# Moving each left operand of the matmuls off the multiple of 512 bytes at which it starts

## The reference, cut to what matters

```
x = x + (u * (W_s v + b)) @ w_out        # u, v = halves of gelu(rms_norm(x) @ w_in), v layer-normed
x = x + (silu(h @ w_gate) * (h @ w_up)) @ w_down          # h = rms_norm(x), width 5632 inside
k, v = rms_norm(h @ w_k), h @ w_v                          # 16 heads of 128
x = x + softmax(q k^T) v @ w_o                             # causal, q = rms_norm(rms_norm(x) @ w_q)
x = x + (silu(h @ w_gate) * (h @ w_up)) @ w_down
```

## Time and profile before

| | |
|---|---|
| median of 3 runs | 2164.18 us (2164.0 to 2165.37) |
| profiled execution: its time | 2164.16 us |
| profiled execution: span, first to last instruction | 2162.4 us |
| busy: PE, PEld | 2140.1 us, 1777.0 us |
| busy: VectorE, ScalarE | 1117.8 us, 998.6 us |
| granted TensorE clock, mean | 0.998 of full |
| instructions | 25371 |

### The profile page before, as it was taken

One profiled execution on the slowest core, in us unless ns is written; L12 is line 12 of the kernel. 1 busy time (PEld: TensorE's weight loads), 2 busy tenths in 40 slices (PEclk: granted clock), 3 DMA queues, 4 the chain that ended last, 5 costly groups with the idle time before them and its releaser, 6 DMA issues.

```text
span 2162.4 us, 25371 instructions
## 1 busy us (share of the span) xinstructions
PE 2140.1 (99%) x9745; PEld 1777.0 (82%) x9745; DVE 1117.8 (52%) x1222; ACT 998.6 (46%) x1229; POOL 29.6 (1%) x37
## 2 busy tenths in 40 slices
PE   7999999999999999999999999999999999999999
PEld 6888888888888888888888888788888888888887
DVE  4566554455444544444556565554554445544443
ACT  5444554444444444444566565454444444443332
POOL 0000000000000000000000000000000000000000
PEclk9999999999999999999999999999999999999999
DMA  8555555555555555554654444455555555555553
GB/s 292 195 165 186 175 186 187 191 194 191 179 193 194 187 182 195 195 192 145 228 188 163 167 167 152 156 195 193 187 186 191 189 186 188 193 188 191 193 193 131
DMA packets 202057, 402.47 MB, mean 186 GB/s; under 512 B 6576, under 2 KB 6672, under 8 KB 201744
## 3 DMA queue, kind: packets, MB, share of 16 engines
q1 hardware_dynamic: 200896, 398.53, 54.4%
q10 hardware_dynamic: 1104, 3.15, 0.4%
HBM read 399.56 MB, written 2.10 MB: 186 GB/s over the span
## 4 chain that ended last, share of the span: by engine, by line
PE 98%; DMA 0%; DVE 0%; issue 0%; ACT 0%; SPq 0%; POOL 0%; ACTq 0%; DVEq 0%
PE acc L904 31%; PE acc L908 31%; PE acc L906 31%; PE tr L931 2%; DMA res<-in_x_dram 0%; PE tr L975 0%; PE tr L1049 0%; PE tr L1039 0%; PE tr L1057 0%; PE acc L931 0%; PE tr L1067 0%; PE tr L1066 0%; PE tr L1048 0%; PE tr L1065 0%; ACT w_hi L342 0%
## 5 line engine op out<-in xcount | busy, mean ns | idle before, releaser
L633 DVE TENSOR_TENSOR w_lo<-raw,w_hi 128x1024 fp32r<-128x1024 f32 x656 | 801.5, 1225 | 873.4 <-ACT w_hi L342 872.8
L342 ACT ACTIVATE w_hi<-raw 128x1024 fp32r<-128x1024 f32 x656 | 692.8, 1060 | 937.8 <-PE acc L908 937.8
L904 PE MATMUL acc<-w_hi,a_hi 128*128 128x512 f32 x2048 | 806.4, 394 | 3.5 <-DVE w_lo L633 3.5
L908 PE MATMUL acc<-w_hi,a_lo 128*128 128x512 f32 x2048 | 799.0, 390 | 0.0
L906 PE MATMUL acc<-w_lo,a_hi 128*128 128x512 f32 x2048 | 798.7, 390 | 0.0
L904 PEld LDWEIGHTS acc<-w_hi,a_hi 128*128 128x128 f32 x2048 | 385.5, 188 | 82.8 <-issue 3.8
L908 PEld LDWEIGHTS acc<-w_hi,a_lo 128*128 128x128 f32 x2048 | 385.4, 188 | 80.9
L906 PEld LDWEIGHTS acc<-w_lo,a_hi 128*128 128x128 f32 x2048 | 385.7, 188 | 78.6
L904 PE MATMUL acc<-w_hi,h_hi 128*128 128x512 f32 x704 | 274.3, 390 | 0.0
L908 PE MATMUL acc<-w_hi,h_lo 128*128 128x512 f32 x704 | 274.0, 389 | 0.0
L906 PE MATMUL acc<-w_lo,h_hi 128*128 128x512 f32 x704 | 273.9, 389 | 0.0
(11 more groups left out here) (110 smaller groups left out, 775.5 us busy)
## 6 DMA issues: line engine op xcount, KB each, us to landing
raw<-in_ffn_w_gate_dram SPq DMA_DIRECT2D x88, 1024.0 KB, 5.0
raw<-in_ffn_w_up_dram SPq DMA_DIRECT2D x88, 1024.0 KB, 5.0
raw<-in_ffn_w_down_dram SPq DMA_DIRECT2D x88, 1024.0 KB, 4.9
raw<-in_a_w_in_dram SPq DMA_DIRECT2D x32, 1024.0 KB, 5.2
raw<-in_a_w_out_dram SPq DMA_DIRECT2D x16, 1024.0 KB, 4.9
raw<-in_w_v_dram SPq DMA_DIRECT2D x16, 1024.0 KB, 4.9
raw<-in_w_k_dram SPq DMA_DIRECT2D x16, 1024.0 KB, 4.9
raw<-in_b_w_q_dram SPq DMA_DIRECT2D x16, 1024.0 KB, 4.8
```

Of the source, the lines that this page charges most:

```text
L342: nc.scalar.activation(dst, src, ACT.Copy).then_inc(hi_split, 1)
L633: nc.vector.tensor_tensor(lo, src, hi, ALU.subtract).then_inc(lo_split, 1)
L904: nc.tensor.matmul(acc[s][t][:, :], hi[:, kb, tok], w_hi[:, slot, k, :], start=kb == 0, stop=False)
L908: ins = nc.tensor.matmul(acc[s][t][:, :], lo[:, kb, tok], w_hi[:, slot, k, :], start=False, stop=kb == HG * n - 1)
```

## The change

Tiles named `pad0` to `pad7`, which nothing reads or writes, are put ahead of each left operand, and the filler `edge_high` is made 256 bytes smaller. No instruction is added, removed or moved; only start addresses change:

| left operand | start, bytes past a multiple of 512: before | after |
|---|---|---|
| a_hi, a_lo | 0, 0 | 128, 256 |
| g_hi, g_lo | 0, 0 | 32, 320 |
| h_hi, h_lo | 0, 0 | 384, 448 |
| o_hi, o_lo | 0, 0 | 96, 224 |

`raw`, `w_hi` and `w_lo` stay where they were. What is allocated behind a pad moves with it: `res`, `stage` and `ident` to 256, `v_nat`, `ln_gain`, `ln_bias`, `w_sT` and `u_nat` to 320, and `val`, `k_nat`, `q_nat`, `kT`, `qT`, `prob` and the others of the attention to 224. Each of the three parts behind `edge_high` begins at the same byte as before, since 256 bytes were added ahead and 256 taken from the filler.

```
+        pads = iter(range(16))
+
+        def pad(size, scope=ctx):
+            sb(f"pad{next(pads)}", [P, size // 4], F32, scope)
+
         sb("edge_low", [P, (-FIRST % LINE) // 4], F32)
         raw = sb("raw", [P, RAW, 2 * HG, CH], F32)
         w_hi = sb("w_hi", [P, RING, HG, CH], F32R)
         w_lo = sb("w_lo", [P, RING, HG, CH], F32R)
+        pad(128)
         a_hi = sb("a_hi", [P, KB, S], F32R)
+        pad(128)
         a_lo = sb("a_lo", [P, KB, S], F32R)
         res = sb("res", [P, TT, D], F32)
...
-        sb("edge_high", [P, (-SMALL % LINE) // 4], F32)
+        sb("edge_high", [P, (-SMALL - 256) % LINE // 4], F32)
...
+            pad(32, part)
             g_hi = sb("g_hi", [P, KB, S], F32R, part)
+            pad(288, part)
             g_lo = sb("g_lo", [P, KB, S], F32R, part)
...
+            pad(384, part)
             h_hi = sb("h_hi", [P, FB, S], F32R, part)
+            pad(64, part)
             h_lo = sb("h_lo", [P, FB, S], F32R, part)
...
+            pad(96, part)
             o_hi = sb("o_hi", [P, KB, S], F32R, part)
+            pad(128, part)
             o_lo = sb("o_lo", [P, KB, S], F32R, part)
```

## The result

| | before | changed |
|---|---|---|
| median | 2164.16 us (2164.0 to 2165.37, 4 runs) | 2218.72 us (2217.04 to 2219.24, 4 runs) |
| profiled span | 2162.4 us | 2215.3 us |
| granted TensorE clock | 0.998 | 0.999 |

What follows compares the result with a forecast made beforehand. The prediction took TensorE's 9024 large matmuls, 226.7 ns each from start to start, to bound the kernel. All terms were 0, so 2164.16 + 0 = 2164.2 us; own range 2160 to 2168, 8-in-10 range 2132 to 2206.

Steps and rivals of the forecast that it cites:

- The sum and what bounds: Whole kernel: TensorE's 9024 large matmuls at 226.7 ns decide; the change adds 0 to 2164.16 us.
- the terms for the small matmuls, ScalarE, VectorE and the DMAs: Work besides the large matmuls, whose tiles move: each term taken as 0; small matmuls at most 3.2 us, DMAs 0.8 us.
- The load: Weight loads of the 9024 large matmuls, from shifted starts: 188 ns each, unchanged, term 0.
- 38.7 ns to spare: Large matmuls: step of 226.7 ns less load of 188 ns; a load slower by less would not show.
- The streams beside it: w_hi and w_lo streaming through the array beside the loads: term 0, ends -120.9 us and as much upwards.
- out of step: Large matmuls: unequal hi and lo distances unsettle load and stream, 26.5 us, or 39.7 us if all three; 24%.
- unsettled stretch of the earlier trace: Nine steps behind small matmuls in the trace before: 231.1 ns each, 4.4 ns more, the price used for the first rival.
- rival of the boundary: Left operands: 512-byte pieces across a boundary cost a second access, 120.9 us, or 19.7 us for 128-byte boundaries; 11%.
- faster: Large matmuls: load and stream collide at equal starts, a distance removes some; 2043.3 us for all, 2140.1 for a fifth; 25%.
- 13.4 ns: Each large matmul: part of the 226.7 ns step beyond 213.3 ns for 512 columns at 2.4 GHz; 120.9 us over 9024.

Runs made afterwards that it cites:

- e4: Kernel before with only the tiles that are no operand of a large matmul moved, as in the changed kernel: 2164.32 us, ratio 0.9999.
- e13: Kernel before with 384 columns streamed instead of 512 in all but the first and last blocks, loads whole, h at distance 128: 1771.52 us.
- e3: Kernel before with every tile, left and right operands alike, 128 bytes past a multiple of 512: 2165.65 us, ratio 1.0003.
- e8: Kernel before with only raw, w_hi and w_lo moved, to 128 bytes past a multiple of 512: 2212.94 us, ratio 1.0222.
- e1: Kernel before with hi and lo at one distance (a 128, g 32, h 384, o 96), right operand at 0: 2213.12 us, ratio 1.0223.
- e11: Kernel before with hi at 0 and lo at 256 in all four products, right operand at 0: 2164.86 us, ratio 1.0.
- e15: Kernel before without its two fillers, so right operand and a start at 128, g, h and o at 192 past a multiple of 512: 2182.73 us, ratio 1.0086.
- e6: Kernel before with hi and lo at small distances, a 16, g 8, o 24 bytes, and h at 96 and 128: 2182.63 us.

## Why the prediction was wrong

The forecast was no change, 2164.2 us, and the range ended at 2206; it is 2218.7.

*The sum and what bounds.* Right. 9024 steps and nothing else carry the difference; the terms for the small matmuls, ScalarE, VectorE and the DMAs were rightly 0 (e4 shows it for the tiles that are not left operands, and no wait grew).

*The load.* Its recorded time is as forecast: 188 ns before and after. The 38.7 ns to spare were no sound reading, though: in e13 the step is 173.3 ns while the loads are recorded with 188 to 189 ns, so a recorded load time does not bound the step. And spare time of the load says nothing of the stream beside it: it is the step from stream to stream that got longer.

*The streams beside it.* Here it failed. The term was put at 0 and measured 52.9 us, 5.9 ns on each of the 9024 matmuls. "I take 0" rested on two observations. The first, one step for left operands at many places, was no test: all these places differ by multiples of 512 bytes, so the distance to the right operand was 0 modulo 256 in every one of them. The trace of before held one value of the variable and could not show its effect. The second, no disturbance by ScalarE and VectorE, was true, but it was about other engines and not about the load and the stream. The Trainium skill's rule (SBUF — State Buffer, section "Who interferes with whom"), that TensorE never waits on anyone, agrees with the trace for ScalarE and VectorE (226.7 ns beside both). For TensorE's own two operands it does not hold as the prediction used it: e3 against e8 and e1 (mean steps in a of 227.0, 232.5 and 232.4 ns) shows that the step depends on the two addresses together.

*The rival "out of step".* It had the sign, and the place as far as the runs show it: TensorE's two operands. Its price with all three loads unsettled was 4.4 ns each, 39.7 us; measured is 52.9 us, 5.9 ns a matmul. Its cause was wrong: the difference between hi and lo is not needed (e1) and can be harmless (e11). What it had right is the kind of thing: the steps run into a pattern that repeats, at distance 0 the even one of 226.7 ns, elsewhere longer and mostly uneven ones with means of 229 to 234 ns. The unsettled stretch of the earlier trace rows, 231.1 ns, looks like a sample of that; no run ties the two together. Its sign, a mean that follows the difference between hi and lo with h least, did not come: h (difference 64) is at 233.3 ns, like a (128), and g (288) is least.

*The rival of the boundary* falls with e3. *The rival "faster"* took the 13.4 ns for a collision which a distance would lessen; no distance did, and by e13 they are the same at 384 and at 512 columns at distance 0. The range's upper end, 2206, came from the first rival's 2203.9 us, and that from the mean of nine unsettled steps. A mean is no upper bound. The longest of the nine is 0.24 us:

```profile
114.05 0.40 PE L904 MATMUL acc<-w_hi,a_hi 128*128 128x512 f32 x1
114.29 0.39 PE L906 MATMUL acc<-w_lo,a_hi 128*128 128x512 f32 x1
```

At that price for every matmul the time would have been some 120 us more; the measured 5.9 ns a matmul lies between the mean and this.

## What to carry to other kernels

In a float32 kernel like this one, with a weight load beside each 512-column stream at the full clock, the start of the left and of the right operand should be equal modulo 256 bytes; it is the distance that counts, not the place, and a few odd tiles ahead of one operand (1088 bytes in e15) are enough to lose it: 0.9% in e15, where three of the four left operands are off, and 2.5% in the changed kernel, where all are. A trace in which all operands lie alike can't tell what another layout would cost; before taking "the same at every place" for evidence, write down by how much the places differ. And a load that seems to have time to spare is no cover for a stream that is at its limit.

## What the runs showed of the hardware that was not expected

- The step of 512-column matmuls with a load each is 226.7 ns where left and right start equal modulo 256 bytes, and 228.9 to 234.1 ns at the other multiples of 32 (means, hi and lo at one distance); at 1.2 GHz three steps are 426.7 ns each at distance 128 (e8) as well as at 0.
- At distance 0, 13.3 ns of it do not shrink with the stream (384 columns: 173.3 ns, of which 160.0 are columns). Loads recorded with 0.19 us start 0.17 us apart there.
- The step is a state, not a fixed price: at 16 bytes the same product ran at 226.7 ns in one phase and at 233.3 ns in another (e6), and with half the load it ran at a mean of 229.7 ns at distance 0.
- Which of the streams a load meets, and by what mechanism their distance acts, the runs do not settle.
